# Hymba decode layer on one core: the order of small steps round the key search, the recurrence gates and the decode keys

## The chip, the core and the metric

One core of a Trainium2 chip runs the whole program. The metric is the device time of one execution in microseconds. Five engines work beside each other, each with its own instruction stream: TensorE (PE; its weight loads PEld), VectorE (DVE), ScalarE (ACT), GpSimd (POOL) and SyncE (SP), which issues most DMAs. They meet in semaphores: `x.wait_ge(s, n)` holds an engine until semaphore `s` has reached `n`, `.then_inc(s, 1)` raises it.

## What is computed

One layer of a hybrid decoder, for a prompt of 1024 tokens and for 8 sequences that decode one token each, with 1024 cached keys apiece. Cut to what matters:

```python
mod = silu(c) @ ada_w + ada_b                       # 6 x 1024: shifts, scales and gates
h = rms_norm(x) * (1 + sc1) + sh1
xr, gr, q, k, v, iq, ik, iw = split(h @ w_in)
# group A: recurrence over the tokens, 512 channels
xc = causal_conv(xr, conv_w, conv_b)                # width 4
r, gi = sigmoid(xc @ wa + ba), sigmoid(xc @ wx + bx)
a = exp(-8 * softplus(-lam) * r)
hr = scan(a, sqrt(1 - a * a) * gi * xc)
out_a = gelu(gr) * hr
# group B: attention over the 256 keys with the highest index score
score = sum_h iw_h * relu(iq_h . ik);  idx = top_k(score, 256)
out_b = softmax(q . k[idx] / 8) @ v[idx]
mix = concat(rms_norm(out_a), rms_norm(out_b)) @ w_out
x = x + g1 * mix
x = x + g2 * (silu(h2 @ w_gate) * (h2 @ w_up)) @ w_down    # h2: norm of x with sc2, sh2
```

## The kernel before

All activations lie feature-major in SBUF (128 partitions by tokens). Every large product is made of three: each factor is split into a high part (rounded to fp32r, a cast on ScalarE) and a low part (the rest, a subtraction on GpSimd for weights and on VectorE for activations), and TensorE adds high x high, high x low and low x high. The order of all work is written out by hand for each engine; there is no planner. These stages matter here:

**Key search, about 125 to 272 us.** The 256th largest score of each query is found bit by bit in 32 rounds `r`. In each, VectorE counts for four tiles (`count`, line 2034, into the scratch `junk`) and ScalarE for three (`signs`, line 1312). Into these rounds other work is laid at fixed bits: `qkv_evac(n)` on ScalarE copies projection group `n` out of its PSUM bank `QKV_BANK[n % 6]` at round `1 + n*16//26`; `unit_evac(u)` copies out unit `u` at round `UNIT_BIT[u]` and adds to it the modulation sums; `ada_row_late(j)` on VectorE copies the row of modulation product `j`, one round after `unit_bit`.

TensorE meanwhile makes 27 projection groups, then 8 **units** (`unit`, line 3045: 72 matmuls, 128 columns of `w_in` for all tokens; 0 to 3 are the recurrence's inputs, 4 to 7 its Gelu branch). Unit 0 uses banks 3 to 5 and waits for `s_pqe` (projection groups evacuated). Behind each unit stand `ada_columns_late` (turns the row that VectorE copied) and `ada_late(j)` (product `j` of the modulation, `adb` holds its weights, loaded by `load_ada`). A unit needs its split weights (`s_wL`, GpSimd's `low(u)`, line 1007) and a free bank (`s_lev`). `load_ada(j)` waits for product `j-1` (`s_adp`), `load_lru(u)` for GpSimd's `low(u-3)`. All loads are issued by SyncE in one order (lines 740 to 762).

GpSimd works through squares and rotations of the heads, `low(3)` to `low(7)` and the convolutions 0 to 2 (`conv`, scratch `gel[:, 2]` and `gel[:, 3]`; done: `s_xc`).

**Gates, about 280 to 340 us.** For each channel tile `c` TensorE makes two gate products, ScalarE takes `gate_r(c)` and `gate_i(c)` (Sigmoid), `decays` (Tanh, Exp), `decay_squared` and `root(c)` (Sqrt); VectorE takes `gated`, `root_input` and `rooted`. ScalarE loads a table whenever the next function lies in another set (ACT_TABLE_LOAD). Units 6 and 7 and the first keys of the attention (`keys_turned`, `first_keys_high`, `first_keys_low`, `q_high`, `q_low`) are laid between.

**Attention loop, about 340 to 488 us.** 16 groups of four heads, with logits, exponentials, transposes and value products.

**Decode keys and mix, about 488 to 552 us.** For each of 8 sequences TensorE turns a page set (`turned_pages(b)`), ScalarE copies it (`page_keys_out(b)` into `kbT[b % 2]`, which needs the logits of `b-2`), TensorE multiplies (`decode_logits(b)`). Beside that, the two groups are normed: VectorE `mix_scaled(c, n)`, ScalarE `mix_high(c, n)`, VectorE `mix_low(c, n)`, for token chunk `c` and feature tile `n` (0 to 3 recurrence, 4 to 7 attention), counted in the order `MIX_ORDER`. `gains` makes the scale of the second norm. Then come `out_group(0)` to `(23)`, the output projection, with the decode probabilities, values (`pvS`) and residuals between the first of them; `high(u)` and `low(u)` split their weights.

**FFN, from about 640 us.** Not touched.

## Time and profile before

| what | value |
|---|---|
| runs | 1322.65 us median (1322.6, 1322.65, 1324.2) |
| profiled execution | 1319.56 us, its span 1317.8 us, 25134 instructions |
| TensorE (PE) busy | 1271.0 us, 96% of the span |
| VectorE, ScalarE, GpSimd busy | 879.8, 679.4 and 696.5 us |
| granted TensorE clock | 0.986 of full speed over the span |
| chain that ended last | TensorE 69%, VectorE 10%, ScalarE 7% |
| HBM | 150 GB/s over the span |

A row of the timeline gives the start in us from the span's start, the length in us, the engine, the line of the kernel, the operation, output and inputs with their shapes, how many instructions were merged (x), and in brackets how long the engine had been idle before and who released it. PE is TensorE, DVE VectorE, ACT ScalarE, POOL GpSimd, SPq SyncE's queue of DMA issues. Matmul records overlap, so a busy TensorE isn't one at its peak, and its idle time is what counts.

### The profile page before, as it was taken

The page shows a single profiled execution, that of the slowest core. Times are in us where ns is not written, and L with a number is a line of the kernel's source. Part 1 is how long each engine was busy: PE and PEld are TensorE (multiplying, and loading weights), DVE is VectorE, ACT ScalarE, POOL GpSimd, SP SyncE. Part 2 cuts the span into 40 slices and gives each one's busy share as a digit, 9 for nine tenths or more (in the row PEclk, how much of TensorE's full clock was granted, in tenths as well). Part 3 has the DMA queues.
Part 4 walks back from the last instruction along what each step waited for, and adds up shares of the span by engine and source line. Part 5 has one row for each costly group of instructions (what it writes and reads, how often), then busy time and mean ns, then how long its engine had stood idle before and what let it go on. Part 6 is the DMA issues. An engine that isn't in the chain of part 4 may idle for free.

```text
span 1317.8 us, 25134 instructions
## 1 busy us (share of the span) xinstructions
PE 1271.0 (96%) x9473; PEld 1150.0 (87%) x9473; DVE 879.8 (67%) x1640; ACT 679.4 (52%) x1163; POOL 696.5 (53%) x438
## 2 busy tenths in 40 slices
PE   6899999999899999999999999999999999999998
PEld 4677997887656655899999999999999999999998
DVE  6777889889689947657983445555555463644595
ACT  5657888949887775445343333333433336211115
POOL 0242448990000002456577878888778857765730
PEclk9799999999899999999999999999999999999999
DMA  9722115452101126455231343434434268999633
GB/s 353 270 69 72 50 33 162 148 184 84 49 17 33 36 78 209 147 172 179 81 128 33 121 169 130 152 112 155 161 129 161 97 245 304 321 339 342 251 129 130
DMA packets 127273, 198.85 MB, mean 151 GB/s; under 512 B 16839, under 2 KB 100111, under 8 KB 116656
## 3 DMA queue, kind: packets, MB, share of 16 engines
q1 hardware_dynamic: 127008, 193.01, 42.4%
q10 hardware_dynamic: 144, 4.23, 0.8%
q8 instruction: 75, 1.23, 0.4%
q14 instruction: 46, 0.38, 0.1%
HBM read 144.07 MB, written 53.18 MB: 150 GB/s over the span
## 4 chain that ended last, share of the span: by engine, by line
PE 69%; DVE 10%; ACT 7%; issue 3%; DVEq 2%; POOLq 2%; DMA 2%; SPq 2%; POOL 1%; ACTq 1%
PE ps L3459 30%; PE ps L3479 15%; PE ps L3323 2%; PE ps L3325 2%; PE ps L3324 2%; PE ps L3154 2%; PE ps L3166 2%; ACT junk L1317 2%; DMA ada_shift<-in_ada_w 1%; DVE junk L2037 1%; PE ps L3143 1%; DVEq L2585 1%; DVE lg L2254 1%; PE ps L2885 1%; ACTq L1319 1%
## 5 line engine op out<-in xcount | busy, mean ns | idle before, releaser
L1010 POOL TENSOR_TENSOR wL<-wraw,wH 128x1024 fp32r<-128x1024 f32 x28 | 69.5, 2483 | 269.8 <-ACT wH L1310 269.5
L3479 PE MATMUL ps<-input,down_H 128*128 128x258 f32 x1120 | 180.6, 283 | 1.5 <-DVE acc L2733 1.5
L3479 PEld LDWEIGHTS ps<-input,down_H 128*128 128x128 f32 x1120 | 154.5, 190 | 2.1 <-issue 1.1
L3459 PE MATMUL ps<-comb,opH 128*128 128x258 f32 x960 | 154.4, 283 | 0.0
L1133 POOL TENSOR_TENSOR opL<-wsum,opH 128x512 fp32r<-128x512 f32 x80 | 124.4, 1564 | 36.8 <-ACT opH L1657 33.5
L1657 ACT CAST opH<-wsum 128x512 fp32r<-128x512 f32 x80 | 49.6, 621 | 168.2 <-PE ps L3459 114.9
L3459 PEld LDWEIGHTS ps<-comb,opH 128*128 128x128 f32 x960 | 132.7, 190 | 0.0
L3459 PE MATMUL ps<-h2H,opH 128*128 128x258 f32 x640 | 129.0, 283 | 0.3 <-DVE h2L L2590 0.3
L3459 PE MATMUL ps<-h2H,opL 128*128 128x258 f32 x640 | 129.0, 283 | 0.0
L3459 PE MATMUL ps<-h2L,opH 128*128 128x258 f32 x640 | 128.6, 282 | 0.0
L2733 DVE TENSOR_TENSOR acc<-ps,acc 128x516 f32<-128x516 f32 x112 | 76.4, 694 | 62.2 <-PE ps L3479 61.7
L1317 ACT ACTIVATE junk<-score,keyX 128x896 bf16<-128x896 f32 (+2 forms) x96 | 106.0, 1106 | 18.8 <-DVE keyX L2108 13.8
L3479 PE MATMUL ps<-input,down_L 128*128 128x258 f32 x560 | 113.1, 283 | 0.0
L1133 POOL TENSOR_TENSOR opL<-raw,opH 128x512 fp32r<-128x512 f32 x60 | 95.0, 1583 | 32.4 <-ACT opH L1657 32.4
L2037 DVE TENSOR_SCALAR_CACHE_REDUCE junk<-score,keyX 128x384 bf16<-128x384 f32 (+5 forms) x138 | 106.2, 826 | 0.2
L3459 PEld LDWEIGHTS ps<-h2H,opH 128*128 128x128 f32 x640 | 99.3, 189 | 0.5 <-issue 0.5
L3459 PEld LDWEIGHTS ps<-h2L,opH 128*128 128x128 f32 x640 | 99.1, 189 | 0.0
L3459 PEld LDWEIGHTS ps<-h2H,opL 128*128 128x128 f32 x640 | 99.0, 189 | 0.0
L3459 PE MATMUL ps<-comb,opL 128*128 128x258 f32 x480 | 96.8, 283 | 0.0
L3479 PEld LDWEIGHTS ps<-input,down_L 128*128 128x128 f32 x560 | 86.7, 190 | 0.0
L2662 DVE TENSOR_TENSOR staged<-gf,staged 128x1032 fp32r<-128x1032 f32 x35 | 60.3, 1723 | 33.1 <-ACT staged L1689 33.0
L3459 PEld LDWEIGHTS ps<-comb,opL 128*128 128x128 f32 x480 | 74.2, 189 | 0.0
(518 smaller groups left out, 3473.2 us busy)
## 6 DMA issues: line engine op xcount, KB each, us to landing
down_inputs<-staged SPq DMA_DIRECT2D x35, 1032.0 KB, 4.8
input<-down_inputs SPq DMA_DIRECT2D x35, 1032.0 KB, 6.9
adb<-in_ada_w SPq DMA_DIRECT2D x8, 2048.0 KB, 8.3
wraw<-in_w_out SPq DMA_DIRECT2D x24, 512.0 KB, 4.4
raw<-in_w_gate SPq DMA_DIRECT2D x10, 1024.0 KB, 6.3
raw<-in_w_up SPq DMA_DIRECT2D x10, 1024.0 KB, 5.1
down_block<-in_w_down SPq DMA_DIRECT2D x5, 2048.0 KB, 10.9
x_feature_major<-x0T ACTq DMA_DIRECT2D x1, 4128.0 KB, 15.4
```

What stands on the lines that cost most here:

```text
L1010: pool.tensor_tensor(lo[:], raw_[:], hi[:].bitcast(F32), ALU.subtract).then_inc(s_wL, 1)
L1133: pool.tensor_tensor(opL[g % OPS][:], operand(v, p), opH[g % OPS][:].bitcast(F32), ALU.subtract).then_inc(s_wL, 1)
L1317: ins = A(junk[0:m, off:off + w], score[0:m, off:off + w], ACT.Sign, scale=-1.0, bias=keyXs[r % 2][0:m, n:n + 1].bitcast(F32), accum_out=c ...
L1657: nc.scalar.copy(opH[g % OPS][:], operand(v, p)).then_inc(s_wH, 1)
L2037: V.tensor_scalar(junk[0:m, off:off + w], score[0:m, off:off + w], thr[0:m, n:n + 1].bitcast(F32), 0.0, op, ALU.add, accum_out=cnt[0:m, n: ...
L2662: V.tensor_tensor(stg[n % 2][:, :, 1, :], down_input(b, p), stg[n % 2][:, :, 0, :].bitcast(F32), ALU.subtract).then_inc(s_aL, 1)
L2733: V.tensor_tensor(two(acc[p][:, m, :]), ps[:, 2 * m:2 * m + 2, 0:HC], two(acc[p][:, m, :]), ALU.add).then_inc(s_dne, 1)
L3154: ins = tr(ps[:, 4 + item % 2, h * P:(h + 1) * P], lg[(GRP * n + h) % NLG][:, k * P:(k + 1) * P], ident)
L3166: ins = mm(ps[par * HD:(par + 1) * HD, 6 + n % 2, 0:2 * P], value, heads[:, par], start=(k == 0), stop=(k == tile_of(n)))
L3323: mm(dst, wH[s][:, k, :], hi, start=(k == 0), stop=False)
L3459: ins = mm(ps[:, sum_bank(v, p) + h, 0:HC], weight[s][:, k, :], token[:, k, h * HC:(h + 1) * HC], start=begins, stop=ends, skip_group_chec ...
L3479: ins = mm(ps[:, 2 * m + h, 0:HC], weight[:, f, cc], tok[:, f, part, h * HC:(h + 1) * HC], start=(f == 0 and weight is hi and part == 0), ...
```

## The change

- `QKV_BANK` gives group `n % 6 = 4` bank 5 and `n % 6 = 5` bank 6 (it was the other way round), and unit 0 waits for 23 evacuated groups, not 24.
- The first modulation row is copied in round 19, not 21 (`ROW_BIT`); the others stay.
- `load_ada(7)` stands ahead of `load_lru(7)`.
- Gate `gi[1]` is written to `root3`, no longer to a scratch row of the convolution, and `gate_i(1)` stands ahead of the wait for the convolutions. `root3` lies where the counts' scratch `junk` lay, so the counts of the last tiles write to its start, with one added drain.
- ScalarE loads the Gelu table and takes `unit_evac(6)` ahead of `root(0)` and `root(1)`.
- `root(2)` and `rooted(2)` stand between the first and the second key copy; `rooted(2)` was behind the query's low part.
- `page_keys_out(6)` and `(7)` each stand ahead of a pair of `mix_high`.
- Two memsets and `gains` move ahead of `squares_added(1, T)`, the memset of `samp2` behind the copy of `lrow`.
- `mix_half(1, 1)` is split: its scaling stands ahead of the copies of the turned probabilities, its low part behind them.

```diff
-QKV_BANK = (0, 1, 2, 3, 6, 5)
+QKV_BANK = (0, 1, 2, 3, 5, 6)
@@
+ROW_BIT = (19, 23, 26, 29)
@@
-        gi = (spare[0][:], gel[:, 2, :], spare[0][:], gel[:, 3, :])
+        gi = (spare[0][:], root3[:], spare[0][:], gel[:, 3, :])
@@ SyncE
             load_ada(ADA_1 + 2)
+            load_ada(ADA_1 + 3)
             load_lru(7)
-            for j in range(ADA_1 + 3, ADA):
+            for j in range(ADA_1 + 4, ADA):
                 load_ada(j)
@@ ScalarE
             gate_r(1)
+            gate_i(1)
             act.wait_ge(s_xc, 4)
-            gate_i(1)
             decays(0)
             decay_squared(0, 2)
             decay_squared(1, 3)
+            A(dsm[:, 7:8], consts[0:64, C_ONE:C_ONE + 1], ACT.Gelu_apprx_tanh)
+            unit_evac(6)
             root(0)
             root(1)
-            unit_evac(6)
             A(dsm[:, 7:8], consts[0:64, C_ONE:C_ONE + 1], ACT.Sigmoid)
@@
             first_keys_high(0)
+            root(2)
             first_keys_high(1)
             q_high(0)
-            root(2)
             root(3)
             first_keys_high(2)
@@
             page_keys_out(5)
             high(U_OUT + 1)
+            page_keys_out(6)
             for n in range(LT, LT + 2):
                 mix_high(0, n)
-            page_keys_out(6)
+            page_keys_out(7)
             for n in range(LT + 2, KD):
                 mix_high(0, n)
-            page_keys_out(7)
             high(U_OUT + 2)
@@ VectorE, count
-                    V.tensor_scalar(junk[0:m, off:off + w], score[0:m, off:off + w], thr[0:m, n:n + 1].bitcast(F32), 0.0,
+                    if n0 < n == SEL_ACT:
+                        dve.drain()
+                    to = off - (SEL[SEL_ACT][3] if n >= SEL_ACT else 0)
+                    V.tensor_scalar(junk[0:m, to:to + w], score[0:m, off:off + w], thr[0:m, n:n + 1].bitcast(F32), 0.0,
                                     op, ALU.add, accum_out=cnt[0:m, n:n + 1])
@@ VectorE, search
                 for u in range(LT):
-                    if unit_bit(u) + 1 == r:
+                    if ROW_BIT[u] == r:
                         ada_row_late(ADA_1 + u)
@@
             first_keys_low(0)
+            rooted(2)
             first_keys_low(1)
             q_low(0)
-            rooted(2)
             rooted(3)
@@ VectorE, mix
+            V.memset(dpT[:, PG * 64:], 0.0)
+            V.memset(ptl[:, 64:96], 0.0)
+            gains(V_LN2, 32)
             squares_added(1, T)
             dve.wait_ge(s_lt, 1)
             V.tensor_copy(lrow[:], ps[0:80, 3, 0:P]).then_inc(s_lte, 1)
+            V.memset(samp2[:], 0.0)
             dve.wait_ge(s_gr, 2)
@@
             mix_half(1, 0)
-            V.memset(dpT[:, PG * 64:], 0.0)
-            V.memset(ptl[:, 64:96], 0.0)
-            V.memset(samp2[:], 0.0)
-            gains(V_LN2, 32)
             dve.wait_ge(s_gr, 4)
@@
             dve.drain().then_inc(s_dpn, 1)
+            for n in range(LT, KD):
+                mix_scaled(1, n)
             dve.wait_ge(s_dpt, 1)
             V.tensor_copy(dpT[:, 0:PG * 64], ps[:, 3, :])
             V.tensor_copy(ptl[:, 0:64], ps[0:NB, 4, 0:64])
             dve.drain().then_inc(s_dpe, 1)
-            mix_half(1, 1)
+            for n in range(LT, KD):
+                mix_low(1, n)
@@ TensorE
-                pe.wait_ge(s_pqe, 24 if u == 0 else NQKV)
+                pe.wait_ge(s_pqe, 23 if u == 0 else NQKV)
```

## Rows read from the trace of the kernel before

**Rows 1.** Table of stages, FFN. Columns: busy us (instructions) per engine, clock, DMA share, GB/s.
```profile
683.00:1317.80 634.80, 629.32 (x5232) 628.11 (x5232) 337.75 (x364) 219.91 (x350) 446.96 (x263) 1.00 0.51 184
```

**Rows 2.** Table of stages, attention loop; busy columns: PE, PEld, DVE, ACT, POOL.
```profile
340.30:488.40 148.10, 139.26 (x865) 88.12 (x865) 119.44 (x278) 115.57 (x241) 0.00 (x0) 0.98 0.15 44
```

**Rows 3.** Waits of PE, 125 to 600 us: us in total, times, longest.
```profile
PE ps L3270 <- ACT kbT L1517: 2.9, 1, 2.9
PE ps L3040 <- DVEq L2083: 2.4, 1, 2.4
PE ps L3053 <- ACT qk L1302: 1.9, 1, 1.9
PE ps L3034 <- DMA adb<-in_ada_w: 1.8, 1, 1.8
```

**Rows 4.** Timeline of ACT (evacuation 22) and PE (start of unit 0).
```profile
190.22 0.37 ACT L1302 COPY qk<-ps 128x256 f32<-128x256 f32 x1
197.95 0.40 PE L3053 MATMUL ps<-hH,lH 128*128 128x344 f32 x1 [1.89 <-ACT qk L1302]
```

**Rows 5.** Timeline of DVE: end of round 19's counts, and the row copy of round 21.
```profile
213.06 0.16 DVE L2089 TENSOR_TENSOR keep<-cnt,ps 128x4 int32<-128x4 f32 x1
224.28 0.81 DVE L2082 COPY mrowb<-ps 128x256 f32<-128x256 f32 x2
```

**Rows 6.** Timeline of PE (modulation products 4 and 7) and SPq (weight loads from 7 on).
```profile
209.39 1.92 PE L3034 MATMUL ps<-adb,cT 128*32 128x512 f32 x16
248.74 41.34 SPq L742 DMA_DIRECT2D adb<-in_ada_w  x4
257.85 3.55 PE L3034 MATMUL ps<-adb,cT 128*32 128x512 f32 x16 [1.78 <-DMA adb<-in_ada_w]
```

**Rows 7.** Timeline of POOL: low parts 5 and 6, last step of convolution 2.
```profile
267.02 4.77 POOL L1010 TENSOR_TENSOR lL<-lraw,lH 128x1024 fp32r<-128x1024 f32 x2 [0.18 <-issue]
293.38 2.38 POOL L1078 TENSOR_TENSOR xr<-xr,gel 128x1032 f32<-128x1032 f32 x1
```

**Rows 8.** Timeline of ACT: first Tanh of `decays(0)`, and `gate_r(2)`.
```profile
299.22 1.16 ACT L1375 ACTIVATE spare<-decay,nsp 128x1032 f32<-128x1032 f32 x1
314.87 1.10 ACT L1355 ACTIVATE decay<-ps,vec 128x1032 f32<-128x1032 f32 x1
```

**Rows 9.** Timeline of ACT: the table load of `root(2)`.
```profile
332.90 1.28 ACT L1370 ACT_TABLE_LOAD   x1
```

**Rows 10.** Timeline of PE and ACT: logits 5; copy of keys 6; logits 6 and 7.
```profile
511.86 1.99 PE L3276 MATMUL ps<-kbT,qb 128*64 128x512 f32 x6
515.56 1.01 ACT L1514 COPY kbT<-ps 128x1024 f32<-128x1024 f32 x1
518.20 5.00 PE L3276 MATMUL ps<-kbT,qb 128*64 128x512 f32 x12
```

**Rows 11.** DVE: timeline of `gains` and an idle place; `mix_scaled(0, 4..7)` by its line (min/median/max ns).
```profile
494.19 1.23 DVE L2290 TENSOR_TENSOR gsq<-gsq 128x1024 f32<-128x1024 f32 x1 [3.31 <-ACT gsq L1562]
509.19 2.21 DVE L1894 TENSOR_SCALAR g1p<-mod 128x72 f32<-128x72 f32 x1
...
L1834 DVE SCALAR_TENSOR_TENSOR attT<-attT,vec,nr x4: 605/606/2793, 511.8 to 515.6; 128x384 f32<-128x384 f32 x4
```

**Rows 12.** Timeline of DVE: the copy of the turned probabilities.
```profile
532.67 0.69 DVE L2487 COPY dpT<-ps 128x512 f32<-128x512 f32 x1 [3.68 <-PE ps L3347]
```

**Rows 13.** Timeline of DVE (`pvS`) and PE (its turning; `out_group(5)`).
```profile
546.20 0.42 DVE L2494 COPY pvS<-ps 128x256 f32<-128x256 f32 x1
546.70 0.44 PE L3367 MATMUL ps<-consts,pvS 128*128 128x128 f32 x2 [0.79 <-DVEq L2495]
552.26 0.45 PE L3323 MATMUL ps<-mixH,wH 128*128 128x384 f32 x1 [0.92 <-POOL wL L1010]
```

**Rows 14.** DVE sums of 1032 elements: timeline, and the page's group in the FFN.
```profile
297.41 1.23 DVE L2127 TENSOR_TENSOR xr<-spare,xr 128x1032 f32<-128x1032 f32 x1
...
L2662 DVE TENSOR_TENSOR staged<-gf,staged 128x1032 fp32r<-128x1032 f32 x35 | 60.3, 1723 | 33.1 <-ACT staged L1689 33.0
```

## Prediction: what the change is expected to do

> **What bounds the kernel now.** I read the page's busy shares, then a table of stages, then what TensorE waited for, then the timeline of each engine round those waits. TensorE is busy for 96% of the span by the page, and in the 635 us of the last stretch, the FFN, for 629 us [rows 1]: nothing in the diff touches that stretch, so it can only be moved as a whole. What can be won is idle time of TensorE ahead of it, and the waits between 125 and 600 us [rows 3] are few and short: 2.9 us for copied decode keys, 2.4 for a modulation row, 1.9 for an evacuated projection, 1.8 for modulation weights; two more of 0.8 and 0.9 lie in the output projection. Behind some of them TensorE is also slow for a while. The attention loop between, 148 us, is paced by VectorE and ScalarE together (119 and 116 us busy [rows 2]); the diff leaves it alone, so I let it pass a shift through unchanged. The sum is made against the profiled execution, 1319.56 us (span 1317.8); the median of the runs shown is 1322.65, 3.1 above, and the difference is applied to that.
>
> **First stretch, up to the attention loop.** (a) `QKV_BANK` with the wait on 23. Unit 0 now needs evacuation 22, not 23. Copy 22 was done at 190.6, while copy 23 came so late that unit 0 started at 197.95, 1.9 us after the projection's end at 196.1 [rows 4]. So that wait goes and everything behind on TensorE moves from 197.95 to about 195.9: -2.0. The swap adds no instruction. (b) `ROW_BIT`: the first row copy moves from round 21 to 19 of the search. Its product follows unit 0 (72 matmuls, 11.4 us from 197.95 to 209.39) and ended at 211.3 (209.39 + 1.92 [rows 6]), with (a) at 209.3; VectorE has counted round 19 at 213.2 [rows 5], so it does not wait, and the copy's 0.8 us is paid there instead of at 224.28 [rows 5]. Round 20 starts 0.8 later, round 22 as before. The 2.4 us wait goes, and so does the slow stretch behind it. Next late: nothing until product 7. TensorE: unit 1 ends 220.8, product 5 at 223.5, unit 2 ends 235.0, product 6 at 237.9. (c) `load_ada(7)` ahead of `load_lru(7)`. The weight load stood behind a load that waited for GpSimd until 248.3, was issued at 248.74 and made TensorE wait until 257.85 [rows 6]. Now it goes out at 237.9 and is there as long after as now, 9.1 us, at 247, while unit 3 runs until 249.4. `load_lru(7)` is now queued behind product 6, earlier than its own wait (248.3), so it loses nothing. The product itself takes 1.92 instead of 3.55 [rows 6], as the clock has not fallen. Unit 4 would start at 252.2 instead of 261.3, 9 us early.
>
> That is not kept. GpSimd's chain of rotations and convolutions runs without a gap and is not moved: its low part for unit 5 ends at 267.02 + 2.4 = 269.4 [rows 7]. TensorE, ready at 266.6, waits 2.9 us there; whether the clock falls isn't shown, so between 0 and the 1.6 us of the product at 257.85, and I take 1. Unit 5 ends near 282 instead of 287. Then the second bound: convolution 2 ends at 295.8 [rows 7]. (d) `gate_i(1)` writes to `root3` and stands ahead of that wait, so its 1.1 us is done when 295.8 comes; decay work starts at 295.9 instead of 299.22 [rows 8]: -3.3. The added drain in the last count costs VectorE 0.1, hidden since VectorE gains 1.1 from earlier gates. (e) Gelu table and `unit_evac(6)` ahead of the roots: still three table loads of 1.28. Squares end at 303.8; unit 6 (11.5 us from about 292.5, plus 0.9 for its columns) is ready at 305, its evacuation ends near 307.2, the roots 3.4 later, the Sigmoid table 1.3 later: gate 2 starts at 312.1 to 312.6 instead of 314.87 [rows 8]: -2.5. Queued behind the new wait are the two roots, and behind them `rooted(0)`, `rooted(1)` and `gate_i(3)`, due at 314.7 and 317: in time. (f) Root 2 between key copies 0 and 1: it needs VectorE's `root_input(2)`, at 328.1 by VectorE's chain (only 1.1 earlier than before), then table and root to 330.5; the second key copy follows at 331.1 and the query copy at 331.6, where they stood at 331.8 and 332.3 with the table load behind them at 332.90 [rows 9]. The Gelu table is loaded at 334.7 to 336, unit 7's evacuation ends at 338.1, and the first logits come at 338.1 instead of 340.3. **First stretch: -2.2**; between -1.0 (clock falls fully, one more copy late) and -3.0.
>
> **Second stretch, decode keys.** Times are those of before. TensorE transposes keys 6 until 511.9, multiplies keys 5 until 513.85, then waits 2.9 us, because ScalarE copies keys 6 only at 515.56, behind two mix casts which wait for VectorE [rows 10]; and the next keys take 5.00 for 12 matmuls where 6 took 1.99 [rows 10], 1 us more. Now the copy of keys 6 stands ahead of the casts: 512.0 to 513.1, in time for 513.85. Keys 7 are turned at 514.9 and copied to 516.1 (casts 4 and 5 fit in between, 513.1 to 514.1, as their scaled input exists by then: next item); logits 6 end at 516.75, logits 7 at 518.7. `out_group(0)` starts at 518.7 instead of 523.13: -4.4. `gains` and the memsets leave a place where they held VectorE from 509.19, 2.21 us for one 72-element instruction with GpSimd running [rows 11], and go to a 3.31 us idle place at 490.9 [rows 11]: 0.8 us, free. So scaling of the attention half starts at 509.7, when the norm is there, 2.1 earlier.
> The rest of the mix: `mix_scaled(1, 4..7)` goes into VectorE's 3.68 us idle place ahead of the probabilities [rows 12]. Queued behind it are the copies that TensorE needs after `out_group(2)`, at 532.5. The four take 2.4 us undisturbed, 4.38 when GpSimd's subtraction falls on one of them (605 ns against 2793 [rows 11]). VectorE is free at 524.6, so they end at 527.0 or 528.9, the copies at 529.8: 2.7 us of slack. The four have left what lies between the probabilities and `pvS`. One subtraction of GpSimd (530.5 to 532.9) still falls there and blocks one instruction: `pvS` is copied at 538.6 if none is hit, at 539.8 if a scaling is, at 540.8 if a low part is; I take 540.4. TensorE wants it at 541.4, so the 0.8 us wait [rows 13] goes. `out_group(5)` waits for GpSimd's part of unit 13, which ended 6.1 us after `pvS` began (546.20 before, its own start at 552.26 after a 0.9 us wait [rows 13]) and hangs on the same chain of residual, square and cast: 546.5 now, where TensorE asks at 546.2. **Second stretch: 552.3 - 546.5 = -5.8**, of which 4.4 are there at `out_group(0)`; between -4.4 (both later waits stay as they are) and -6.1 (TensorE alone sets it).
> A rule that speaks against this: the Trainium skill, GPSIMD Engine Reference, 1. Specifications, says that GpSimd's SBUF interfaces are shared with VectorE, with contention for VectorE instructions that have two SBUF inputs; that is scaling and low part alike. The trace agrees: 605 against 2793 ns for the one, and for plain sums of 1032 elements 1.23 us alone and 1.72 on average in the FFN, where GpSimd is busy [rows 14]. By the rule `pvS` would come at 540.8, and the stretch would bring -5.4; without it -6.1.
> Sum: -2.2 -5.8 = -8.0. 1319.56 becomes 1311.6, and 1322.65 becomes **1314.7 us**.
>
> **Rivals.** *A. Only the second stretch counts.* GpSimd's chain sets both ends of the first stretch, and VectorE's chain there gains only 1.1 us; if the clock falls at 266.6 and the second key copy is late, or if the attention loop swallows the shift, 0 of 2.2 arrives: 1316.9. For: the loop's engines wait for each other. Against: it has no outside due time. *B. The wait moves.* VectorE's scaling is blocked once more ahead of `dpT` or `pvS`, so both later waits stay and one of 1 to 2 us is added: second stretch -3, total -5, 1317.5. For: the 2793 ns. Against: 2.7 us of slack. *C. It does not do what it says.* Another resource holds the decode keys (the copy of keys 7, or the mix's low half at `out_group(0)`, due at 520.7 and ready at 518), and A holds too: -2, 1320.7. *D. Slower.* One mechanism: TensorE's clock. The attention loop begins beside idle time, and its granted clock is 0.98 over the whole [rows 2]. If the shifted start leaves it at the lower level of 1.2 GHz for longer, each us of matmul work that is on the path costs 0.85 us more (1.92 against 3.55 [rows 6]). The gain is gone at 9.4 us of such work; it is slower by 0.2% from 12.5; with 20 us it is 1322.65 - 8 + 17 = 1331.6. Against: the same kinds of work follow in the same order, and idle time gets less.
>
> **Numbers.** Forecast 0.58, A 0.18, B 0.12, C 0.08, D 0.04. A measurement tells 0.2%, 2.6 us, from no change: 1320.0 is the border. Faster: the forecast, A, B = 0.88, with C just beyond the border; same 0.08; slower 0.04. The range takes in the forecast with its bounds (-4.4 - 1.0 gives 1317.3, -6.1 - 3.0 gives 1313.6), A and B with 1 us about them, and leaves C and D out: 1312.5 to 1319.2.
>
> **What would show it.** In the changed kernel: unit 0 starts on the heels of the projection (195.9); no wait at the columns at 221 and none for `adb`; a new wait of about 3 us for GpSimd's `lL` near 267; `decay` tanh at 295.9; first logits at 338; no wait of TensorE for `kbT`, `out_group(0)` 6 to 7 us earlier than at 523.1; the wait at `pvS` gone. Wrong if the first logits stay at 340, if `mixL` or `wL` becomes the releaser of `out_group(0)`, or if the granted clock of the attention loop falls below 0.95.

## The result, and the profile after

The changed kernel takes 1313.93 us (median of 5 executions, 1311.41 to 1315.75) where the kernel before takes 1322.6 (1320.28 to 1324.2) on the same chip: a ratio of 0.9940, 95% interval 0.9929 to 0.9951. Forecast were 1314.7 us, in a range of 1312.5 to 1319.2. The profiled execution took 1313.93 us, its span 1312.1, granted clock 0.987.

I cut every trace of this study at the same six instructions. The columns are differences between starts in the timeline of PE: start of the span to the first matmul of the projection; from there to the first logits (A); to the first turned page of decode keys (B, the attention loop); to `out_group(0)` (C); to the turning of `pvS` (D); to the FFN (E); to the end (F). All in us:

| kernel | start | A | B | C | D | E | F |
|---|---|---|---|---|---|---|---|
| before | 119.4 | 220.86 | 148.46 | 34.37 | 23.57 | 127.12 | 644.0 |
| changed | 118.8 | 219.02 | 150.13 | 29.98 | 22.63 | 126.19 | 645.4 |
| changed again (e4) | 118.1 | 219.87 | 148.78 | 29.81 | 22.62 | 126.24 | 644.0 |
| second stretch only (e1) | 119.3 | 222.02 | 149.51 | 30.41 | 22.62 | 126.36 | 645.0 |
| first stretch only (e2) | 120.4 | 220.80 | 148.78 | 34.36 | 23.58 | 127.12 | 644.0 |
| order of key copies only (e3) | 121.2 | 220.77 | 149.90 | 30.13 | 23.62 | 127.14 | 644.0 |
| without the early load (e5) | 119.9 | 222.68 | 150.17 | 30.45 | 22.64 | 126.18 | 644.0 |
| without banks and row (e6) | 119.4 | 218.40 | 149.99 | 29.81 | 22.63 | 126.17 | 645.0 |
| fillers at gate 2 (e7) | 121.7 | 219.02 | 149.48 | 31.47 | 22.64 | 126.17 | 644.0 |
| scaling moved (e8) | 122.0 | 225.90 | 151.27 | 30.06 | 22.63 | 126.19 | 644.0 |
| `gains` left in place (e9) | 118.0 | 219.88 | 148.75 | 29.88 | 22.63 | 126.20 | 644.0 |
| without the split (e10) | 121.2 | 219.67 | 148.76 | 29.80 | 23.59 | 127.08 | 644.9 |
| fillers in the loop (e11) | 122.4 | 219.12 | 148.14 | 29.80 | 22.62 | 126.23 | 644.0 |
| both fillers, no banks and row (e12) | 122.1 | 218.87 | 148.13 | 29.80 | 22.63 | 125.55 | 644.3 |

Over executions with the same code there D repeats to 0.05 us and E to 0.2 (e12's is 0.6 less, and why isn't shown). C is 29.80 to 29.88 in six traces with the new order of the key copies, and 29.98 to 31.47 in the six whose granted clock was at the lower level for 3.4 us round its start or in it (the changed kernel, e1, e3, e5, e7, e8; in e7 from 502.5 to 506.0 us). The start varies by 4.4 us without any edit, B by 1.7 (2.8 with e8), and F by 1.5. So one trace doesn't show a gain in its span: the changed kernel's is 5.7 us shorter, made of start -0.7, A -1.8, B +1.7, C -4.4, D -0.9, E -0.9, F +1.4. What the change moved is A, C, D and E: -8.1.

A varies too. Three traces have the old code up to the first logits (before, e1, e3: 220.77 to 222.02, mean 221.2), five the whole new code (changed, e4, e2, e9, e10: 219.02 to 220.80, mean 219.8). On average the new code is 1.4 us earlier, and a difference between two single traces can be anything from 0 to 3 us.

**Waits of TensorE.** Waits of PE in the changed kernel (what waits, for whom: us in total, times, longest):

```profile
PE ps L3163 <- ACT pT L1457: 3.2, 8, 0.6
PE ps L3069 <- ACT decay L1357: 3.0, 2, 2.2
...
PE ps L3062 <- POOL lL L1012: 2.6, 1, 2.6
...
PE ps L3488 <- issue: 1.3, 1, 1.3
PE ps L3152 <- ACTq L1338: 1.0, 1, 1.0
PE ps L3049 <- DVEq L2089: 1.0, 1, 1.0
PE ps L3119 <- DVE kT L2216: 0.8, 1, 0.8
```

All four waits of [rows 3] are gone. In their place stand 2.6 us for GpSimd's low part (forecast 2.9), 2.2 us at L3069 for ScalarE's gate 2, where it was 0.5 (not forecast), 1.0 at L3049 for a modulation row and 0.8 at L3119 for VectorE's low part of the first keys (neither forecast). The 1.0 us at L3152, ahead of the first logits, stood there before with 1.2.

**First stretch.** Timeline of the changed kernel, PE: columns for product 4, unit 4, unit 5, gate products of chunk 2 and of chunk 3.

```profile
219.82 0.95 PE L3049 MATMUL ps<-consts,mrowb 128*128 128x9 f32 x8
252.11 0.43 PE L3062 MATMUL ps<-hH,lH 128*128 128x344 f32 x1
268.88 0.43 PE L3062 MATMUL ps<-hH,lH 128*128 128x344 f32 x1 [2.57 <-POOL lL L1012]
306.75 3.74 PE L3069 MATMUL ps<-xr,wbd 128*128 128x344 f32 x12
312.70 3.74 PE L3069 MATMUL ps<-xr,wbd 128*128 128x344 f32 x12 [2.20 <-ACT decay L1357]
```

Unit 4 starts 9.2 us earlier than in the kernel before, of which 0.7 is the earlier start of the whole, so 8.5 where 9.1 was forecast, and unit 5 waits for GpSimd. ScalarE and GpSimd in the same kernel: first Tanh; Gelu table; evacuation of unit 6; `gate_r(2)`; table of `root(2)`; low parts 5 and 6; end of convolution 2.

```profile
295.33 1.16 ACT L1377 ACTIVATE spare<-decay,nsp 128x1032 f32<-128x1032 f32 x1 [1.27 <-POOLq L1081]
303.21 1.28 ACT L1398 ACT_TABLE_LOAD   x1
305.07 1.03 ACT L1332 ACTIVATE gel<-ps 128x1032 f32<-128x1032 f32 x1 [0.36 <-PE ps L3049]
311.55 1.10 ACT L1357 ACTIVATE decay<-ps,vec 128x1032 f32<-128x1032 f32 x1
...
326.41 1.28 ACT L1372 ACT_TABLE_LOAD   x1
...
266.48 4.70 POOL L1012 TENSOR_TENSOR lL<-lraw,lH 128x1024 fp32r<-128x1024 f32 x2 [0.18 <-issue]
292.75 2.43 POOL L1080 TENSOR_TENSOR xr<-xr,gel 128x1032 f32<-128x1032 f32 x1
```

Against [rows 8] the Tanh comes 3.9 us and `gate_r(2)` 3.3 us earlier, of which 0.7 is the earlier start. The Tanh hangs, as said, on GpSimd's convolution 2, which ends at 295.2. `gate_r(2)` hangs on the Tanh's chain and, for a last 0.36 us, on the columns of unit 6.

**Second stretch.** Timeline of the changed kernel: ScalarE's copies of keys 6 and 7 with the casts between; TensorE's logits 6 and 7 and `out_group(0)`; the turning of `pvS`; `out_group(5)`; VectorE's scalings in their new place, and its copy of `pvS`.

```profile
511.28 1.01 ACT L1517 COPY kbT<-ps 128x1024 f32<-128x1024 f32 x1 [0.22 <-PE ps L3279]
512.28 0.92 ACT L1535 CAST mixH<-attT 128x384 fp32r<-128x384 f32 x2
514.23 1.01 ACT L1517 COPY kbT<-ps 128x1024 f32<-128x1024 f32 x1 [1.02 <-PE ps L3279]
...
514.12 3.83 PE L3285 MATMUL ps<-kbT,qb 128*64 128x512 f32 x12
517.88 0.45 PE L3332 MATMUL ps<-mixH,wH 128*128 128x384 f32 x1
540.52 0.38 PE L3376 MATMUL ps<-consts,pvS 128*128 128x128 f32 x2
545.18 0.45 PE L3332 MATMUL ps<-mixH,wH 128*128 128x384 f32 x1
...
523.51 4.35 DVE L1837 SCALAR_TENSOR_TENSOR attT<-attT,vec,nr 128x384 f32<-128x384 f32 x4
539.08 0.42 DVE L2503 COPY pvS<-ps 128x256 f32<-128x256 f32 x1
```

The 12 matmuls that took 5.00 us [rows 10] take 3.83 without a gap behind them; `out_group(0)` comes 5.3 us earlier (the forecast named 6 to 7 as a sign; the longer loop of this trace makes the difference), `out_group(5)` 7.1, and neither `pvS` nor `out_group(5)` has a wait in brackets, against [rows 13].

### The profile page after: what moved, and what is told of

The parts are those of the page before. It is cut to its first block, busy times and chain, and to the rows that moved or that the text cites. A ratio compares the mean times of both kernels' runs of the same rounds, so it can differ in the third digit from the quotient of the medians.

```text
span 1312.1 us, 25134 instructions
## 1 busy us (share of the span) xinstructions
PE 1269.6 (97%) x9473; PEld 1152.6 (88%) x9473; DVE 879.6 (67%) x1640; ACT 679.4 (52%) x1164; POOL 699.7 (53%) x438
## 4 chain that ended last, share of the span: by engine, by line
PE 66%; DVE 15%; ACT 6%; DVEq 4%; issue 3%; ACTq 2%; SPq 2%; DMA 1%; POOL 0%
PE ps L3468 30%; PE ps L3488 15%; DVE junk L2043 3%; ACT junk L1319 3%; PE ps L3175 2%; ACTq L1321 2%; PE ps L3163 2%; PE ps L3332 2%; PE ps L3334 2%; PE ps L3333 2%; DMA ada_shift<-in_ada_w 1%; PE ps L3152 1%; DVEq L2594 1%; PE ps L3285 1%; DVE lg L2260 1%
```

## Experiments

The kernel before ran beside each set on the same chip: 1321.51 us for e1 to e4, 1320.81 for e5 to e8, 1320.82 for e9 to e11, 1321.94 for e12 (medians).

### e1 and e2: each stretch alone

e1 has only the edits behind the attention loop, e2 only those ahead of it:

```diff
             page_keys_out(5)
             high(U_OUT + 1)
+            page_keys_out(6)
             for n in range(LT, LT + 2):
                 mix_high(0, n)
-            page_keys_out(6)
+            page_keys_out(7)
...
+            gains(V_LN2, 32)
             squares_added(1, T)
...
+            for n in range(LT, KD):
+                mix_scaled(1, n)
             dve.wait_ge(s_dpt, 1)
```

> The kernel before with the second stretch of the change alone (page_keys_out order, gains and memsets, mix_scaled(1, 4..7) ahead of the probabilities). Theory (the two stretches add): -5.8 us, between -5.4 and -6.4, 0.9956; out_group(0) 4.4 us earlier and out_group(5) 5.8 to 6.1 us earlier than before. Rival B (the wait moves behind VectorE's blocked scaling): -3 us, with both later waits still there.

> The kernel before with the first stretch alone (banks, row copy, load order, gate 1, Gelu first, root 2). Theory: -2.2 us at the first logits and at the end, 0.998. Rival A (the first stretch does not arrive): first logits 2 us earlier, but 0 to -0.7 us at the end, the rest given back in the attention loop or behind it.

Measured: e1 1314.59 us, ratio 0.9944 (0.9932 to 0.9956); e2 1320.28, 0.9987 (0.9976 to 0.9999). By medians -6.9 and -1.2, by the table -5.7 for e1 in C to E and -0.06 for e2 in A. So the second stretch carries nearly all. The interval of e2 holds the forecast of -2.2 and rival A's -0.7 alike. Why e2's trace shows nothing stands in its waits and clock. PE of e2: gate products of chunk 3; then the table of stages (length, PE busy, granted clock, DMA share, GB/s) for e2, for the changed kernel and for e4:

```profile
314.04 6.77 PE L3066 MATMUL ps<-xr,wbd 128*128 128x344 f32 x12 [3.22 <-ACT decay L1357]
312.00:322.00 10.00, 7.96 (x21) 0.66 0.44 144
```

```profile
312.00:322.00 10.00, 9.30 (x50) 1.00 0.41 131
```

```profile
312.00:322.00 10.00, 9.84 (x42) 0.83 0.34 109
312.16 5.43 PE L3069 MATMUL ps<-xr,wbd 128*128 128x344 f32 x12 [2.21 <-ACT decay L1357]
```

In e2 unit 6 starts 5.7 us earlier than in the kernel before (172.40 us behind the first projection matmul, against 178.10), and unit 7 no earlier (199.95 against 199.91): a wait of 3.2 us for gate 2 lies between, and behind it TensorE ran at 1.2 GHz and needed 6.77 us for 12 matmuls that take 3.74 at 2.4 GHz. In e4 the clock fell there too, for 3.4 us (unit 7 at 199.02), in the changed kernel's own trace it didn't, with the same wait of 2.20 us (197.27). Against the one trace of the kernel before A is -1.8 where the clock holds, -1.0 to -1.2 where it falls for 3.4 us (e4, e9, e10) and -0.1 where it falls for 6.8 (e2).

### e3: the order of the key copies alone

```diff
             high(U_OUT + 1)
+            page_keys_out(6)
             for n in range(LT, LT + 2):
                 mix_high(0, n)
-            page_keys_out(6)
+            page_keys_out(7)
             for n in range(LT + 2, KD):
                 mix_high(0, n)
-            page_keys_out(7)
```

> The kernel before with the order of page_keys_out(6) and (7) alone. Theory: this order carries the 4.4 us at out_group(0), and the waits of 0.8 and 0.9 us ahead of out_group(4) and (5) stay: -4.4 us, 0.9967. Rival (gains and memsets carry it, since the casts in front of the copies waited for VectorE): -2 us or less.

Measured: 1317.56 us, 0.9967 (0.9954 to 0.9979), -4.0 by medians; C 30.13 instead of 34.37, -4.2; D and E as in the kernel before. PE of e3 keeps the wait at `pvS`:

```profile
545.60 0.44 PE L3367 MATMUL ps<-consts,pvS 128*128 128x128 f32 x2 [0.82 <-DVEq L2495]
```

So 4.2 us of the forecast 4.4 are there, from two moved lines, and the 1.7 to 1.9 us of D and E aren't theirs.

### e4: the whole change again

The diff is the change itself.

> The changed kernel again, on the chip of the three others. Theory: -8.0 us, 0.994, the sum of the two stretches. Rival (they overlap): less than the sum of the two stretches measured alone by over 1 us. Its trace also shows whether the 1.25 us halt of TensorE near 1135 us and the low clock near 485 us come again.

Measured: 1313.7 us, 0.9945 (0.9932 to 0.9958), -7.8. The parts, -1.2 and -6.9, add up within what can be told. Neither the halt of TensorE near 1135 us nor the low clock near 485 us of the changed kernel's trace comes again.

### e5: without the early load of modulation weights

```diff
             load_ada(ADA_1 + 2)
-            load_ada(ADA_1 + 3)
             load_lru(7)
-            for j in range(ADA_1 + 4, ADA):
+            for j in range(ADA_1 + 3, ADA):
                 load_ada(j)
```

> The whole change without the earlier load of modulation weights 7. Theory (this load is the step that carries the first stretch): its product waits again, unit 4 starts near 261 instead of 252 us, unit 5 near 275 instead of 269, and the 2.6 us wait for GpSimd's low part for unit 5 is gone; unit 6's columns come late enough that gate 2 is no earlier than before, and the first logits lie 220.5 to 221 us behind the first projection matmul as in the kernel before (220.86), not 219.0. The second stretch is the same. So 1.8 to 2 us more than the whole change. Rival (each step carries a share of its own): the evacuation of unit 6 ahead of the roots and root 2 between the key copies still bring their part, the first logits come at 219.5 to 220, and it costs 1 us or less.

Measured: 1317.5 us, 0.9966 (0.9954 to 0.9978), 3 to 4.5 us more than the whole change (against e4 by the ratios 2.8 and by the medians against the kernel before beside each 4.5; against e6, on the same chip, 3.3). A is 222.68, later even than in the kernel before. PE and ACT of e5: the product; evacuation of unit 6.

```profile
258.47 3.62 PE L3042 MATMUL ps<-adb,cT 128*32 128x512 f32 x16 [5.39 <-DMA adb<-in_ada_w]
310.78 1.03 ACT L1331 ACTIVATE gel<-ps 128x1032 f32<-128x1032 f32 x1 [1.55 <-PE ps L3048]
```

TensorE, made earlier by the other steps, waits 5.4 us for a load that still goes out late, and at half clock. Units 5 and 6 start within 0.3 us of where they did before the change (156.3 and 178.4 us behind the first projection matmul), and the evacuation of unit 6, now ahead of the roots, makes ScalarE wait 1.55 us for it, so that unit 7 comes 1.9 us later than before: a step of the change that costs where the load isn't early. The load carries the first stretch, as the theory said, but its size, 1.8 to 2 us, was too small, because (e) needs the load too and costs without it.

### e6: without the swap of banks and the earlier row copy

```diff
-QKV_BANK = (0, 1, 2, 3, 5, 6)
+QKV_BANK = (0, 1, 2, 3, 6, 5)
...
-                    if ROW_BIT[u] == r:
+                    if unit_bit(u) + 1 == r:
...
-                pe.wait_ge(s_pqe, 23 if u == 0 else NQKV)
+                pe.wait_ge(s_pqe, 24 if u == 0 else NQKV)
```

> The whole change without the swap of banks and without the earlier row copy. TensorE loses the 2.0 us wait at unit 0 and the 2.4 us wait at the first row copy again. Theory (GpSimd's convolution 2, at 295.8 us, is the bound behind which the first stretch's gain is cut off): both are absorbed by the 2.6 us wait for GpSimd ahead of unit 5 and by the slack of the decay work, and the first logits come at most 0.4 us later than 219.0 us behind the first projection matmul; the whole time is that of the whole change within 0.5 us. Rival (TensorE is the bound): 2 to 4.4 us are lost and the gain of the first stretch is gone.

Measured: 1314.24 us, 0.9954 (0.9939 to 0.9969), not to be told from the whole change. A is 218.40, below every trace of the whole change (219.02 to 220.80). The table of stages round unit 5, in the changed kernel and in e6:

```profile
268.00:276.00 8.00, 7.12 (x35) 0.79 0.70 255
```

```profile
268.00:276.00 8.00, 8.00 (x58) 1.00 0.55 183
```

What the two steps win ahead of it is spent waiting for GpSimd: unit 5 starts 150.13 us behind the first projection matmul with them and 150.96 without. The clock falls behind that wait in the changed kernel's trace, and unit 6 starts at 173.77 with them and 173.03 without. In e2, e7 and e11, which have both steps, the clock had already fallen ahead of that wait, from 238 to 244 us, and not behind it; unit 5 starts at 150.1 to 150.3 there too and unit 6 at 172.2 to 172.4. No gain of steps (a) and (b) is to be seen here, neither in A nor in the time.

### e7: fillers at gate 2

```diff
             gate_products(2, 1, 3)
+            for _ in range(4):
+                mm(ps[:, 7, 0:256], ident, consts[:, 0:256], start=True, stop=True)
             pe.wait_ge(s_gs, 5)
```

> The whole change with four more matmuls of 256 columns, whose result nobody reads, between unit 6 and the gate products that wait for ScalarE's gate 2 (the 2.2 us wait that I had not priced). Theory (the gain of the first stretch is lost in some executions because TensorE's clock falls behind this wait, at 313.7 to 320.6 us): with the fillers, which take some 0.5 us of the wait, unit 7 starts 23.5 us behind unit 6, the granted clock shows no low stretch between 312 and 322, and the first logits lie 219.0 us behind the first projection matmul; 0 to 1.7 us less than the whole change. Rival 1 (the fall does not hang on this wait): the low stretch is there as before in some executions, and the time is that of the whole change within 0.5 us. Rival 2 (more activity draws a fall elsewhere): the low stretch moves to a later place and the time is the same or longer.

Measured: 1312.94 us, 0.9937 (0.9924 to 0.9950); by medians -7.9, where e4 had -7.8. The four took 1.9 us, not 0.5, and left 1.50 of waiting. The stretch from 312 to 322 us ran at full clock:

```profile
312.00:322.00 10.00, 8.50 (x42) 1.00 0.56 187
```

Of the nine traces with the first stretch's order and without these fillers, the clock fell at this place in six (e2, e4, e8 to e11) and held in three (the changed kernel, e5, e6); with them it held in two of two (e7, e12). It fell in both traces where the wait was 3.2 us (e2, e11) and in four of the seven where it was 2.2 to 2.3. That agrees with the theory, but two traces don't show it, and the time gained can't be told from nothing.

### e8: GpSimd's scaling moved behind convolution 2

```diff
             conv(0)
-            scaled(2)
-            pool.drain().then_inc(s_qkr, 1)
             low(4)
...
             conv(2)
+            scaled(2)
+            pool.drain().then_inc(s_qkr, 1)
```

> The whole change with GpSimd's scaling for the third head pair moved from ahead of its low part 4 to behind convolution 2. Theory (GpSimd sets unit 5 and the decays, VectorE's chain comes next): the low part for unit 5 ends near 265 instead of 269.4 us, the 2.6 us wait of TensorE for it is gone, convolution 2 ends near 291.7, and the decay work starts near 292 instead of 295.3; but VectorE's root inputs and unit 6's columns then set gate 2, which comes at most 1 us earlier than 311.5, and the first logits gain 0.5 us or less. Rival (GpSimd's convolution is the bound down to the logits): the 3 us pass through, and the whole time is 2.5 to 4 us below the whole change. Slower would be: the scaling, now late, makes the rotated keys late for the first logits.

Measured: 1316.6 us, 0.9978 (0.9962 to 0.9993), more than the whole change by 3.6 us in medians beside the kernel before, which neither theory expected. The wait for GpSimd ahead of unit 5 went, as expected, but in this trace VectorE wasn't ready with the row that is turned behind unit 5. DVE and PE of e8: first step of VectorE's own convolution, one of its sums over 8 elements, the row copy; the columns.

```profile
276.16 2.93 DVE L2121 TENSOR_SCALAR conv_sum<-xr,vec 128x1024 f32<-128x1024 f32 x1
280.57 2.35 DVE L1837 SCALAR_TENSOR_TENSOR conv_sum<-stT,vec,conv_sum 128x8 f32<-128x8 f32 x1
286.76 0.76 DVE L2088 COPY mrowb<-ps 128x256 f32<-128x256 f32 x2 [0.18 <-issue]
...
287.60 1.88 PE L3049 MATMUL ps<-consts,mrowb 128*128 128x9 f32 x8 [4.93 <-DVEq L2089]
```

and the first of these in the changed kernel, with the operation behind it:

```profile
272.85 0.82 DVE L2121 TENSOR_SCALAR conv_sum<-xr,vec 128x1024 f32<-128x1024 f32 x1
273.94 2.16 DVE L1837 SCALAR_TENSOR_TENSOR conv_sum<-xr,vec,conv_sum 128x1024 f32<-128x1024 f32 x1
```

The same operation takes 2.93 us in e8, beside a subtraction or sum of GpSimd's from 276.12 to 278.54, and 0.82 in the changed kernel, where GpSimd was at other work. GpSimd's chain, 4 us earlier, meets VectorE's operations in other places. Three of them take longer than alone (2.93 us for 0.82, 2.35 for 0.22, 2.07 for 1.28), in e7 one (2.16 for 1.28) and in e4 two; VectorE's five sums behind the first step take 7.2 us instead of 5.2 in e7 or 6.0 in e4, so the row is ready 11.4 us after the first step, in e7 7.2; TensorE waits 4.9 us, and its clock falls for 10.2. The executions of e8 fall into two groups, seven from 1314.7 to 1316.8 and five from 1321.4 to 1323.9, and the profiled one, 1323.85, is of the second; so the meeting isn't there each time. What decides it isn't shown, nor why the first group, with a median of 1316.0, is itself 3 us slower than the change by the kernel before beside each.

### e9 and e10: `gains` left in its place; no split of `mix_half(1, 1)`

```diff
-            V.memset(dpT[:, PG * 64:], 0.0)
-            V.memset(ptl[:, 64:96], 0.0)
-            gains(V_LN2, 32)
             squares_added(1, T)
...
             mix_half(1, 0)
+            V.memset(dpT[:, PG * 64:], 0.0)
+            V.memset(ptl[:, 64:96], 0.0)
+            V.memset(samp2[:], 0.0)
+            gains(V_LN2, 32)
```

```diff
-            for n in range(LT, KD):
-                mix_scaled(1, n)
             dve.wait_ge(s_dpt, 1)
...
-            for n in range(LT, KD):
-                mix_low(1, n)
+            mix_half(1, 1)
```

> The whole change with gains and its memsets left where they were (behind mix_half(1, 0)). Theory (their place costs, since one 72-element instruction is held for 2.2 us while GpSimd works, but VectorE has slack up to the probabilities): out_group(0) starts 29.8 to 30.0 us behind the first turned page as with the whole change, and what is lost comes later, at pvS, at most 0.8 us (pvS 22.6 to 23.4 us behind out_group(0)); the time is that of the whole change within 1 us. Rival (the scaled inputs of the mix casts hang on it, so that the copy of keys 7 behind casts 4 and 5 is late again): out_group(0) comes 1 to 2 us later and the gain of the new order of the key copies shrinks from 4.2 to 2 to 3 us.

> The whole change with mix_half(1, 1) in one piece behind the copies of the probabilities, as before. Theory (the split is what takes the two later waits away): out_group(0) is where it is in the whole change, pvS starts 23.4 to 23.6 us behind it instead of 22.6, the FFN 127.1 behind pvS instead of 126.2, so 0.8 to 1.8 us more than the whole change. Rival (the two later waits went because gains moved): pvS and the FFN stay at 22.6 and 126.2, and nothing is lost.

Measured: e9 1314.81 us, 0.9959 (0.9946 to 0.9972); C, D and E as in the whole change within 0.1 us. By medians that is -6.0, where e11, which has the whole change, had -6.5 on the same chip, and e4 -7.8 on another; the cuts are the sharper measure. So moving `gains` brings nothing that can be seen. DVE of e9 has the 2.2 us instruction again and makes them up before anyone asks:

```profile
507.08 2.20 DVE L1897 TENSOR_SCALAR g1p<-mod 128x72 f32<-128x72 f32 x1
509.67 4.40 DVE L1837 SCALAR_TENSOR_TENSOR attT<-attT,vec,nr 128x384 f32<-128x384 f32 x4
```

In the changed kernel the same four scalings start 9.0 us ahead of `out_group(0)`, in e9 6.9; so the forecast 2.1 us are there. They take 5.87 us there and 4.40 in e9. The rival saw the chain rightly: in e9 ScalarE waits 1.55 us for them ahead of the casts, and the copy of keys 7 stands behind (513.46, the turned keys being there at 512.8). But TensorE still multiplies keys 6 then, and only 0.1 us of it arrives at `out_group(0)`.

e10: 1316.35 us, 0.9963 (0.9951 to 0.9974), D 23.59 and E 127.08: the 1.0 and 0.9 us of the kernel before come back. By medians it is -4.5. PE of e10:

```profile
542.97 0.44 PE L3373 MATMUL ps<-consts,pvS 128*128 128x128 f32 x2 [0.79 <-DVEq L2501]
548.53 0.44 PE L3329 MATMUL ps<-mixH,wH 128*128 128x384 f32 x1 [0.92 <-POOL wL L1012]
```

So the split takes both later waits away, and the rival, that `gains` did, is out.

### e11: fillers at the start of the attention loop

```diff
             q_transposed(1)
+            pe.wait_ge(s_kl, 3)
+            for _ in range(2):
+                mm(ps[:, 7, 0:256], ident, consts[:, 0:256], start=True, stop=True)
             pe.wait_ge(s_lev, NU_LRU)
             for g in range(AHEAD * GRP):
                 logits(g)
+                mm(ps[:, 7, 0:P], ident, consts[:, 0:P], start=True, stop=True)
             pe.wait_ge(s_lmod, 1)
-            pe.wait_ge(s_kl, 3)
```

> The whole change with matmuls whose result nobody reads at the start of the attention loop: two of 256 columns (0.9 us) in the 1.05 us wait ahead of the first logits, and one of 128 columns behind each logit group of the first two heads, where TensorE waits 0.3 us each. The loop's start ran at half clock for 6.8 to 10.2 us in every trace so far, whichever edit it had. Theory (the fall hangs on these waits): with the fillers the granted clock stays at full level up to 350 us, and the loop from first logits to first turned page takes 147 us or less instead of 148.5 to 150.1; 1.5 to 3 us less than the whole change. Rival 1 (the fall hangs on what the loop does after, or is not set by idle time of this size): the low stretch is there as before, 148.5 to 150.1 us. Rival 2 (the fillers stand in the way of VectorE-paced logits): 1 us longer.

Measured: 1314.36 us, 0.9955 (0.9942 to 0.9968), by medians -6.5, so the forecast gain of 1.5 to 3 us over the whole change (-7.8 in e4) isn't there. The stretch from 337 to 352 us in the changed kernel and in e11:

```profile
337.00:352.00 15.00, 12.35 (x58) 0.66 0.25 72
```

```profile
337.00:352.00 15.00, 13.36 (x96) 1.00 0.18 51
```

In all twelve traces without these fillers the clock is at its lower level for 6.8 or 10.2 us here; in both with them (e11, e12) it isn't. So the fall hangs on TensorE's short waits of 0.3 to 1.0 us in this place: shown. What it costs is less than I expected: B is 148.14 instead of 148.46 to 148.78 where 6.8 us were slow, and 149.5 to 151.3 where a second slow stretch came later in the loop. The forecast of 147 or less was wrong by 1.1, which goes with VectorE and ScalarE pacing this loop [rows 2]. Whether a later fall lengthens the loop or an unevenness of the loop brings the fall isn't shown.

### e12: what the experiments point to

```diff
-QKV_BANK = (0, 1, 2, 3, 5, 6)
+QKV_BANK = (0, 1, 2, 3, 6, 5)
...
             gate_products(2, 1, 3)
+            for _ in range(4):
+                mm(ps[:, 7, 0:256], ident, consts[:, 0:256], start=True, stop=True)
...
+                mm(ps[:, 7, 0:P], ident, consts[:, 0:P], start=True, stop=True)
```

> The whole change without the swap of banks and the earlier row copy, and with both sets of matmuls whose result nobody reads: in the wait for gate 2 and at the start of the attention loop. Theory (what decides between executions is where TensorE's clock falls, and the wait for GpSimd ahead of unit 5 goes when TensorE is later): no low stretch between 260 and 360 us, first logits 218.4 to 219.0 us behind the first projection matmul, the loop 148.1 us, the second stretch as in the whole change; against the whole change's trace (219.87 and 148.78) 1.5 to 2.1 us less, so 9 to 10 us below the kernel before, 1311 to 1312.5. Rival (the fillers only move the fall, or delay the gate products, as they put unit 7 24.5 instead of 23.5 us behind unit 6 in the trace with the first set): first logits at 219.5 to 220 and the time is that of the whole change, 1313.5 to 1314.5.

Measured: 1312.45 us (1310.4 to 1313.36), 0.9921 (0.9904 to 0.9937), 9.5 below the kernel before beside it. The table of stages of e12:

```profile
268.00:276.00 8.00, 8.00 (x59) 1.00 0.06 8
305.00:312.00 7.00, 7.00 (x50) 1.00 0.00 0
312.00:322.00 10.00, 9.53 (x41) 1.00 0.81 263
337.00:352.00 15.00, 12.82 (x92) 1.00 0.20 56
```

No low clock in any of them; the wait for gate 2 is down to 0.47 us; A is 218.87 and B 148.13, as forecast. It is the fastest of all kernels here, by 0.2% below the changed one; but the two intervals overlap between 0.9929 and 0.9937, so that this beats the change is likely and not shown.

## Why the prediction was right, point by point

**The sum.** Forecast were -2.2 and -5.8, measured by the table -1.8, -1.0 or -0.1 for A, and -6.3 and -6.4 (the changed kernel, e4) for C to E. The total fits in part by luck: the second stretch was too small by about half a us, and the first too large by 0.4 to 2.1, by 0.8 on the mean of the traces.

**(a), (b) banks and row copy.** The waits went as said, and unit 0 starts on the heels of the projection. That the -2.0 doesn't survive GpSimd was said too; in e6 nothing is lost without both. "Next late: nothing until product 7" was wrong by one wait of 1.0 us for the row of product 5, behind unit 2, which costs nothing for the same reason.

**(c) the load.** Unit 4 at 252.1, or 252.8 with the start taken off (forecast 252.2), the wait for GpSimd 2.6 us (2.9). The cost of the clock there was mis-sized: I took 1 us, and unit 6 follows unit 5 by 23.6 us instead of 22.1, so 1.5 in this trace, but 0 in e2, e7 and e11. e5 confirms that this step carries the stretch. (d), (e) and (f) weren't taken out one by one.

**(d), (e), (f) ScalarE.** With the start taken off, `gate_r(2)` is 2.6 us earlier (forecast 2.5). The step that failed is what I left out: with unit 6 ready early and gate 2 bound by ScalarE, TensorE has a wait of 2.2 us at L3069 where it had 0.5 us. I followed ScalarE's chain and took it that TensorE only passes time. The wait itself costs nothing, as ScalarE sets the pace there, but the clock that falls behind it in six of nine traces does. That "whether the clock falls isn't shown" applied here as to the wait ahead of unit 5. And from unit 7 on, VectorE's key copies cap the rest: the new 0.8 us wait for `kT` (1.3 in e7) stands in the traces where unit 7 is early (196.6 to 197.3 us behind the first projection matmul: the changed kernel, e6, e7) and not in those where it is later (198.0 or more).

**The attention loop.** "It passes a shift through unchanged" holds for the mean: B has no tie to the edits (e1, e3 and e5 vary as the whole change does). In one trace it is uncertain by 1.7 us, which I hadn't put in the sum. In the changed kernel's trace it took back nearly all of A, which would look like rival A; e4, same code, doesn't have it.

**Second stretch.** The order of the key copies: forecast -4.4, measured -4.2 (e3) to -4.6 (C of e4, where the clock didn't fall in that stretch). The split: forecast 0.8 for `pvS` and 0.6 for `out_group(5)`, measured 1.0 and 0.9 (e10). The second was mis-sized since I let GpSimd's part of unit 13 end 0.3 us after TensorE asks; it starts at 542.71 in the changed kernel, so by [rows 7]'s 2.4 us it is done at 545.1, when TensorE comes at 545.18. So the bound without any wait, -6.1, was the nearer one. `gains`: I gave it the earlier scalings; they come, but only 0.1 us of them is needed (e9).

**The rule on shared interfaces.** The trace shows it as the forecast counted it: one scaling of the four in the new place is blocked (4.35 us for the four against 2.2 undisturbed), one low part as well (4.16 against 1.97), and the copy of `pvS` starts at 539.08, 1.4 us ahead of TensorE's wish. The Trainium skill, GPSIMD Engine Reference, 1. Specifications, states contention for VectorE instructions in a 2-port perf mode or with two SBUF inputs; the forecast took up only the second. Instructions with one tensor input are held here as well: `gains` (2.2 us for 72 elements beside GpSimd, 0.18 in its new place) and the `TENSOR_SCALAR` of e8 (0.82 against 2.93). Whether they ran in such a mode no run here shows. The rule's result of -5.4 for the stretch didn't come about, as the blocked instructions lay in slack.

**Rivals.** A is out, though weakly: five traces with the new code have their first logits 1.4 us earlier on average than three with the old, and the timed gain of e2 is 0.01 to 0.24%. B and C are out by D, E and C of the table. D is out at its price: in the changed kernel the loop was at half clock for 10.2 us and once more for 3.4, and took 2.0 us longer than e12's, which never was. At rival D's price of 0.85 us for each us of matmul work those 13.6 us, which hold at most 7.4 us of such work, would have cost some 6. Its sign, a granted clock of the loop below 0.95, didn't show: it was 0.96.

## What to carry to other kernels

Take waits away from the last bound backwards: two steps of six in the first stretch only fed a wait for GpSimd, and one (`gains`) a slack nobody used, while two moved lines brought 4 of the 8 us. After moving a chain forward, list the new waits of TensorE too, since its clock can fall behind them (here behind single waits of 2.2 to 3.2 us, and among short ones of 0.3 to 1.0), and a few matmuls into a free bank may hold it. And judge a stretch by cuts at fixed instructions, over several executions: here the start, one loop and lone halts vary by 1 to 4 us each.

## What the runs showed of the hardware that I had not expected

- The same kernel with the same wait of 2.2 us (the changed kernel and e4) had its granted clock at 2.4 GHz behind it once and at 1.2 GHz for 3.4 us the other time. So such a wait doesn't settle whether the clock falls.
- VectorE operations with a single tensor input take longer beside GpSimd's two-input ones: 2.93 us against 0.82 for 1024 elements (e8), 2.2 against 0.18 for 72 (`gains`).
- In four traces (the changed kernel, e1, e6, e10) TensorE stopped once for 0.7 to 1.3 us behind 600 us with nothing to wait for. In the changed kernel it is this row of PE, and F is 1.4 us longer than in most traces; its cause isn't shown.

```profile
1136.06 0.72 PE L3488 MATMUL ps<-input,down_H 128*128 128x258 f32 x4 [1.25 <-issue]
```

- The start of the kernel, up to the first matmul of the projection, varies from 118.0 to 122.4 us between executions, with the same code there. It is the largest single part of what separates two traces here.
